# Neighbourhood attention on one Trainium2 core: the probabilities become TensorE's stationary operand and the values, with two columns of ones, move

## The reference

```python
s_loc = jnp.einsum('bnqhd,bknchd->bhnqkc', q_r, k_band).astype(jnp.float32) * scale
s_loc = jnp.where(in_win[:, :, None, :], s_loc + bias, -jnp.inf)
s_ctx = jnp.einsum('bnqhd,bmhd->bhnqm', q_r, kc).astype(jnp.float32) * scale
s = jnp.concatenate([s_loc.reshape(...), s_ctx], axis=-1)
p = jax.nn.softmax(s, axis=-1).astype(v.dtype)
...
o = (jnp.einsum('bhnqkc,bknchd->bnqhd', p_loc, v_band)
     + jnp.einsum('bhnqm,bmhd->bnqhd', p[..., n_loc:], vc))
```

## Time and profile before

| what | value |
|---|---|
| median of 3 runs | 2772.48 us (2771.65 to 2773.15) |
| span of the profiled execution | 2769.1 us |
| PE, DVE, ACT busy over the whole span | 94%, 79%, 55% |
| chain that ended last | nearly all PE lines of the experts |
| `attend`, from its first score to its last store's issue | 371.3 to 588.6 us |
| time per 16 steps in its middle | 53.7 us |

### The profile page before, as it was taken

One profiled execution on the slowest core, in us unless ns is written; L12 is line 12 of the kernel. 1 busy time (PEld: TensorE's weight loads), 2 busy tenths in 40 slices (PEclk: granted clock), 3 DMA queues, 4 the chain that ended last, 5 costly groups with the idle time before them and its releaser, 6 DMA issues.

```text
span 2769.1 us, 34578 instructions
## 1 busy us (share of the span) xinstructions
PE 2611.0 (94%) x13665; PEld 2202.2 (80%) x13665; DVE 2199.2 (79%) x2029; ACT 1511.2 (55%) x1409; POOL 139.8 (5%) x159
## 2 busy tenths in 40 slices
PE   7999989989999799929999999999999999999997
PEld 2778878878998787828888888888888888888885
DVE  5684269959887656589898888888888888898887
ACT  3432146633221212237777777777777777777774
POOL 0010000000111000000000000000000000000000
PEclk9999999999999999959999999999999999999999
DMA  7498743345887763269999999999999999999994
GB/s 265 155 314 310 234 98 71 97 160 196 281 265 260 269 218 114 100 242 381 382 366 382 391 376 366 383 390 376 364 391 389 370 367 395 386 366 381 387 378 178
DMA packets 206014, 816.61 MB, mean 295 GB/s; under 512 B 31967, under 2 KB 89671, under 8 KB 127712
## 3 DMA queue, kind: packets, MB, share of 16 engines
q1 hardware_dynamic: 182228, 694.82, 67.0%
q0 software_dynamic: 23472, 119.56, 12.7%
q10 hardware_dynamic: 158, 0.07, 0.0%
HBM read 747.00 MB, written 67.39 MB: 294 GB/s over the span
## 4 chain that ended last, share of the span: by engine, by line
PE 52%; ACT 2%; issue 2%; DVE 1%; DVEq 0%; ACTq 0%
PE moe_ps_gate L2126 18%; PE moe_ps_up L2126 16%; PE moe_ps_y L2116 16%; PE moe_ps_h L2097 2%; ACT moe_w_hi L2167 1%; PE moe_ps_x L2089 1%; DVE raw L2289 0%; ACT moe_xt_hi L2160 0%; DVE moe_w_lo L2219 0%; DVE moe_h L2240 0%; ACT moe_sl L2180 0%; DVE raw L2276 0%; PE moe_ps_gate L2150 0%; PE moe_ps_gate L2152 0%; PE moe_ps_up L2150 0%
## 5 line engine op out<-in xcount | busy, mean ns | idle before, releaser
L2219 DVE TENSOR_TENSOR moe_w_lo<-raw,moe_w_hi 128x2048 fp32r<-128x2048 f32 x528 | 1207.6, 2291 | 159.6 <-ACT moe_w_hi L2167 158.9
L2167 ACT ACTIVATE moe_w_hi<-raw 128x2048 fp32r<-128x2048 f32 x528 | 1010.9, 1919 | 379.1 <-PE moe_ps_gate L2126 127.7
L2126 PE MATMUL moe_ps_up<-moe_w_hi,moe_xt_hi 128*128 128x512 f32 (+1 forms) x768 | 292.4, 381 | 0.0
L2126 PE MATMUL moe_ps_gate<-moe_w_hi,moe_xt_hi 128*128 128x512 f32 (+1 forms) x768 | 289.1, 376 | 1.4 <-DVE moe_xt_lo L2210 1.4
L2126 PE MATMUL moe_ps_gate<-moe_w_hi,moe_xt_lo 128*128 128x512 f32 (+1 forms) x768 | 286.4, 373 | 0.0
L2126 PE MATMUL moe_ps_up<-moe_w_hi,moe_xt_lo 128*128 128x512 f32 (+1 forms) x768 | 286.3, 373 | 0.0
L2126 PE MATMUL moe_ps_gate<-moe_w_lo,moe_xt_hi 128*128 128x512 f32 (+1 forms) x768 | 286.1, 372 | 0.0
L2126 PE MATMUL moe_ps_up<-moe_w_lo,moe_xt_hi 128*128 128x512 f32 (+1 forms) x768 | 285.8, 372 | 0.0
L2116 PE MATMUL moe_ps_y<-moe_w_hi,moe_ht_hi 128*128 128x512 f32 x704 | 218.5, 392 | 0.0
L2116 PE MATMUL moe_ps_y<-moe_w_lo,moe_ht_hi 128*128 128x512 f32 x704 | 217.0, 389 | 0.0
L2116 PE MATMUL moe_ps_y<-moe_w_hi,moe_ht_lo 128*128 128x512 f32 x704 | 217.0, 389 | 0.0
(11 more groups left out here) (276 smaller groups left out, 3913.5 us busy)
## 6 DMA issues: line engine op xcount, KB each, us to landing
raw<-in_w_moe SPq DMA_DIRECT2D x528, 1024.0 KB, 7.1
hyena_g_parts<-gw_d POOLq DMA_DIRECT2D x64, 1024.0 KB, 6.2
proj_w_mod<-in_w_mod SPq DMA_DIRECT2D x32, 512.0 KB, 7.6
gw_d<-proj_g_parts POOLq DMA_DIRECT2D x16, 1024.0 KB, 7.3
w_in<-in_w_in SPq DMA_DIRECT2D x12, 1024.0 KB, 8.5
norm_w_mod<-in_w_mod SPq DMA_DIRECT2D x16, 512.0 KB, 6.1
proj_g_raw<-in_w_in SPq DMA_DIRECT2D x16, 512.0 KB, 9.9
hyena_h_parts<-hq_d POOLq DMA_DIRECT2D x16, 512.0 KB, 8.3
```

Source lines behind the costliest of these rows:

```text
L2126: mm = pe.matmul(ps, hp[:, e % 2, k, :], wp[:, r, :], start=(k == 0 and x == 0), stop=(k == KD - 1 and x == 2))
L2167: act.activation(w_hi[:, g % PARTS], raw[:, g % RAW], ACT.Copy).then_inc(hi_ready, 1)
L2219: dve.tensor_tensor(w_lo[:, g % PARTS], raw[:, g % RAW], w_hi[:, g % PARTS].bitcast(F32), ALU.subtract).then_inc(lo_ready, 1)
```

## The change

`product` swaps its operands: the turned probabilities (128 keys x 128 queries) are stationary, and 66 columns of `v_tok` move: the 64 values of the head and two of the ones beside them. The result has queries on partitions: 64 values and the sum twice, in 66 columns. `normalize` then takes the reciprocal of one column (128 x 1) and multiplies 128 x 64 elements by that per-partition scalar into a new buffer `na_q`, where the two heads of a pair lie side by side for each query tile. As `na_t` must still have head dimensions on partitions, 32 transposes are added on TensorE (`turn_na`, one for each pair and query tile, both heads at once) and 32 copies on VectorE (`move_na`). `turn_na` of step s belongs to unit s-4 and is issued for the second head's units only; it waits until `normalize` of that unit is done. Two memsets at the start move behind the preparation of the first head, and the store of a pair now waits for the copies.

```diff
-        inverse = m.sb("inverse", [P, 2, P])
+        inverse = m.sb("inverse", [P, 2])
+        na_q = m.sb("na_q", [P, TT, P])
...
+        def pair_done(step):
+
+            g = step - 4
+            if not 0 <= g < ALL or g % UNITS < TT:
+                return None
+            return g // UNITS, g % TT
...
+        def na_spot(i):
+            return ps_o[:, i % 2, 2 * P:3 * P]
...
-                    sp.wait_ge(used, UNITS * (j + 1) + 2)
+                    sp.wait_ge(na_moved, TT * (j + 1))
...
-                    return v_tok[:, tile, j, hh:hh + 2, :].rearrange("p x d -> p (x d)")
+                    at = (2 * HD - 2) * hh
+                    return v_tok[:, tile, j, :, :].rearrange("p x d -> p (x d)")[:, at:at + HD + 2]
+
+                def turn_na(step):
+                    done = pair_done(step)
+                    if done is None:
+                        return
+                    j, i = done
+                    pe.wait_ge(used, UNITS * j + TT + i + 3)
+                    pe.transpose(na_spot(i), na_q[:, i, :], ident[:]).then_inc(na_turned, 1)
 
                 def product(j, n):
...
+                    moved = pairs_before(UNITS * j + n - 1)
+                    if moved > 0:
+                        pe.wait_ge(na_moved, moved)
...
-                        mm = pe.matmul(ps_o[:, n % 2, 0:P], head_and_ones(tile, j, n // TT), prob_t[:, n % 2, b, :],
+                        mm = pe.matmul(ps_o[:, n % 2, 0:HD + 2], prob_t[:, n % 2, b, :], head_and_ones(tile, j, n // TT),
                                        start=(x == 0), stop=(x == len(todo) - 1))
...
                         turn_probs(j - 1, UNITS + s - 2)
+                    turn_na(UNITS * j + s)
                     if now:
                         scores(j, s)
...
-                dve.memset(keep["w3"][FC:P, :], 0.0)
-                dve.memset(keep["h2"][FC:P, :], 0.0)
...
                 make_table(0, 0)
+                dve.memset(keep["w3"][FC:P, :], 0.0)
+                dve.memset(keep["h2"][FC:P, :], 0.0)
...
-                    dt.then_wait(dve.reciprocal(inverse[head, n % 2], ps_o[total, n % 2, 0:P]))
-                    dve.tensor_tensor(na_t[head, j, i * P:(i + 1) * P], ps_o[head, n % 2, 0:P], inverse[head, n % 2],
-                                      ALU.mult).then_inc(used, 1)
+                    by = inverse[:, n % 2:n % 2 + 1]
+                    dt.then_wait(dve.reciprocal(by, ps_o[:, n % 2, total:total + 1]))
+                    dve.tensor_scalar(na_q[:, i, hh * HD:(hh + 1) * HD], ps_o[:, n % 2, head], by, None, ALU.mult
+                                      ).then_inc(used, 1)
+
+                def move_na(step):
...
+                    dve.wait_ge(na_turned, TT * j + i + 1)
+                    dve.tensor_copy(na_t[:, j, i * P:(i + 1) * P], na_spot(i)).then_inc(na_moved, 1)
 
                 def at_step(j, s, now, before):
                     if now:
                         maxima(j, s)
+                    move_na(UNITS * j + s)
+                    if now:
                         if 2 <= s % TT <= 5 and j + s // TT < PAIRS:
```

More of the change, by code:

```diff
@@ L832, in attend, with pairs_before @@
             sems(n) for n in ("q_high", "k_high", "q_split", "k_split", "tables", "scored", "max_ready", "exps", "turned"))
-        copied, filled, used, zeros = (
-            sems(n) for n in ("probs_copied", "filled", "used", "zeros"))
+        copied, filled, used, zeros, na_turned, na_moved = (
+            sems(n) for n in ("probs_copied", "filled", "used", "zeros", "na_turned", "na_moved"))
         PAIRS, UNITS = HEADS // 2, 2 * TT
+        ALL = PAIRS * UNITS
+        def pair_done(step):
[3 more added lines that the diff above has]
+            return g // UNITS, g % TT
+        def pairs_before(g):
+            return TT * (g // UNITS) + max(g % UNITS - TT, 0)
+        def na_spot(i):
+            return ps_o[:, i % 2, 2 * P:3 * P]
         def blocks(i):
@@ L928, in _ @@
                     at_step(PAIRS, s, False, True)
+                turn_na(ALL + 3)
             @block.scalar
@@ L1044, in normalize @@
                     i, hh = n % TT, n // TT
-                    head, total = (slice(x * HD, (x + 1) * HD) for x in (hh, 1 - hh))
+                    head, total = (slice(0, HD), HD) if hh == 0 else (slice(2, HD + 2), 0)
                     dve.wait_ge(filled, UNITS * j + n + 3)
@@ L1074, in _ @@
                     at_step(PAIRS, s, False, True)
+                move_na(ALL + 3)
 PH = 8
```

## The result

| | median, us | runs |
|---|---|---|
| before | 2772.07 (2770.44 to 2773.77) | 6 |
| changed | 2781.99 (2779.01 to 2788.94) | 6 |

The changed kernel takes 1.0041 times the time of the kernel before (95% interval 1.0030 to 1.0051): slower by about 10 us, against 9 forecast. The sum came out; two of its parts, the periods and the clock, did not, and they nearly cancelled.

A forecast was written before the change was run, and what follows sets the result against it. PE's own work was taken as the floor, with waits added while VectorE prepares heads. Terms 7.05 + 1.2 - 0.25 + 0.9 = +8.9 us took 2772.48 to 2781; range 2769 to 2790, the forecast's own 2776 to 2787.

The forecast's parts named there:

- the periods: Windows of 16 steps in the middle of attention: each 56.05 us against 53.70, 2.35 longer, three times, +7.05.
- last four steps: End of attention, no preparation: the wait for `normalize` makes them 13.43 us against 12.22, +1.2.
- from the mask load to step 11: Beginning of attention: memsets against an earlier `low_q` +0.6, steps 4 to 10 about 0.85 less, together -0.25 us.
- tail: End of the stage: three `turn_na` 0.3, one waiting some 0.8, product loads giving 0.2 back, +0.9 us.
- rival 4: Dearer: stalls at table steps lower the granted clock, or each hand-over costs 0.2 more; 2787 us and above, chance 0.07.
- the loop: Steps 12 to 19: scores, maxima, copy, preparation, `normalize`, `turn_na`, next scores in a closed chain; 31.95 us from scores 11 to 19.
- 0.9 for ScalarE: Eight steps after scores of 19: added because ScalarE's query and key splits precede its copy; bounds 0 and 1.6 us.
- The product: PE's 832 pairs of load and matmul: spacing set by the weight load, 111 to 107 ns each, 3.3 us less.
- the second rival: Product spacing on PE follows its moving columns, 57 ns each; total change 0, so 2772 us; chance 0.07.
- The first rival: VectorE's relief decides, wait at `turn_na` short: 16 steps take 48.2 us, 2757 us in all; chance 0.13.
- Its own test on the plain steps: Steps without preparation: chain behind the scores, 2.41 us, must take less than PE's product and transposes, 2.32.
- The start: Before the first maxima: memsets add 2.9 us, `low_q` starting earlier saves 2.3, +0.6.

The follow-up runs named there:

- both orders: Changed kernel with `turn_na` issued behind the scores on PE and `normalize` ahead of preparation on VectorE: 2759.18 us, ratio to the kernel before 0.9961.

## Why the prediction was right, and where it was not

**The mechanism held.** PE waits at L925 for L1081 in the steps named: 2.32 in step 14 (2.4 said), 1.46 in 19 (within the 0.9 to 1.8 said), 0.55 and 0.71 in 12 and 13 (under the 0.9 said), and no wait on PE's rows in 15 to 18. In the second and third period the wait of step 14 is 1.97. In steps 4 to 8 of the first pair, where none was said, there is one: 0.68 in step 4, for ScalarE's copy. Two more signs came out lower than said: the periods (54.63 and 54.23, not 56) and DVE's busy time in one (37.59, not 41). VectorE was relieved by more than forecast, L1049 and L1050 with 79.6 us against L1080, L1081 and L1090 with 37.8, and the kernel still lost. Putting `turn_na` behind the scores, or `normalize` ahead of preparation, takes the loss away.

**That 2781 came so close to 2781.99 is luck in good part: two errors of opposite sign.** By terms, in the profiled execution:

| term | predicted | measured |
|---|---|---|
| three periods, clock at 1.00 | +7.05 | about +2.4 (54.63, 54.23, and 54.4 for the third) |
| last four steps | +1.2 | +0.4 (12.61 against 12.22) |
| from the mask load to step 11 | −0.25 | −0.3 |
| ahead of the stage | 0 | −0.3 |
| tail | +0.9 | +1.3 (11.39 against 10.09, from the transposes that open the last unit's step) |
| clock | 0, in rival 4 only | +5.7 |
| behind the stage | 0 | +1.4 |

The sum is +8.9 on the one side and, without rounding, +10.7 on the other. Without the clock it would be +5.0; the three periods alone cost about a third of what I gave them. The window from the transposes of step 11 began at 405.37 and now does at 404.83, which are the two −0.3.

**Where the loop was priced too high.** From the `turn_na` of step 12 to that of step 19 I had 27.69 (4.35 + 5.71 + 12.88 + 4.75); it is 26.91: 4.02, 5.86, 12.37 and 4.66. `normalize` is 0.49, as worked out (0.166, a gap of 0.04 and 0.284, in the fence above 418.64 to 419.13). The narrow steps gave most of the difference, 3.09 each in place of 3.22; PE's rows show no wait in them. Maxima and copy together occupy 1.46 (414.62 to 416.08) where I added 1.33 and 0.29: in these rows the next operation starts before a short one has ended (415.88 against 415.75 + 0.21), so the durations of rows must not be summed where starts can be subtracted. `turn_na` itself takes 0.08 of PE (409.31 to 409.39) and not 0.11. The table was off to the other side: it holds `normalize` up 2.56 (416.08 to 418.64), since the reciprocal stood 0.57 behind the halves of `edged`; I had 2.21.

**The other term that failed is "0.9 for ScalarE".** The rest of the period is 27.7 (54.63 − 26.91) against 28.4. In the period of the earlier trace rows PE had waited 4.0 us for ScalarE's copy; in the changed kernel's first period it never does. What fits is that the waits of the earlier trace rows were VectorE's lateness handed on by ScalarE, as the chain of my own first paragraph said, and that they went when VectorE was relieved; I then priced the same delay once as VectorE's and once more as ScalarE's. No run tests this by itself. The whole 0.9 was not gained: from the scores of step 19 to those of step 27 (436.31 to 460.04) PE took 23.73, 0.5 more than the 23.2 that I had for its own work.

**The clock.** That the stalls of 2 us let it fall had a chance of 0.07, with only the clock of 1.00 in the earlier trace rows against it. But those rows held no pause of 2 us like the new ones at `turn_na`; the longest of the earlier trace rows is 1.6. None of the eleven timed runs of the changed kernel has a mean granted clock over 0.973, the lowest of the kernel before in the first group, and filling the pauses brings it back. In both profiled executions this was the most expensive part of the change, and I had it as a side case.

**The product** was right within 2 ns a load: 14 loads from 414.30 to 415.82 are 108.6 ns each, 107 said, and the experiment with 128 columns rules the second rival out. **The first rival** was wrong for this order of work and right for another: its 48.2 and 2757 come near the 48.83 and 2759.18 of both orders. Its own test on the plain steps, a chain of 2.41 against PE's 2.32, was as close as it looked: they took 3.09, where PE's own work had been put at 3.07. What decided was the preparation in the loop. **The start** of +0.6 was +1.0 by both kernels that have it: the memsets hold the first maxima up by 3.5 (9.99 less 6.51), where I had 2.9. The steps behind, up to step 11, gave 1.2 back where I had 0.85. **Open** is the 1.4 us behind the stage: none of the kernels was made for it, and it is within what executions differ by.

## What to carry to other kernels

Relieving an engine is worth nothing while another engine's next start waits in order behind that engine's last item. Before moving work, follow the new wait round: if scores lead to maxima, maxima to `normalize`, and `normalize` back to the next scores, everything queued between is paid in full; put the signalled item ahead of the preparation, and the waiting one behind what it does not need. And price a new pause of PE twice, once as its length and once as the clock that may fall behind it.

## What the runs showed of the hardware that was not expected

- Waits of TensorE of 1.5 to 2.3 us, in a stage where it is busy 92% of the time (197.45 of 213.90), came with a fall of the granted clock to 0.50, for 3.4 to 6.8 us, in six of the twelve cases in two executions. The same waits in other periods of the same executions were followed by none. The falls cost 5.7 us in the first profiled execution, and 10.8 us of the median in the later group. Thirty short transposes in each of the first three pairs, whose result is overwritten, kept the clock at 1.00 in the profiled execution and took those 10.8 us away.
- The fall does not always begin at the same distance from the wait: at 527.2 it came 0.5 us before the wait had ended, at 420.1 it came 1.7 us behind a wait's end (418.38), with PE busy in between.
- In the kernel before, the stage has waits of up to 1.6 us and a clock of 1.00. The kernel with `turn_na` behind the scores had a fall behind a wait of 1.15 us, and none behind its waits of 1.52 and 1.16. No number here separates the pauses that are followed by a fall from those that are not.
- A float32 product with 128 x 128 weights costs 108 ns with 66 columns moving and 111 with 128, in the same step of two kernels that differ in nothing else. Over all 832 products the stage was 1.2 us longer with 128 columns: here next to nothing was to be gained from narrowing the moving side alone.
